# Recurrence of a two-block network: crossing products go in two turns that interleave straight blocks of one head pair with across blocks of the other

## What is computed

```python
def wkv7_scan(r, decay, k, v, kk, a):
    def step(S, inp):
        r_t, w_t, k_t, v_t, kk_t, a_t = inp
        s_kk = jnp.einsum('bhij,bhj->bhi', S, kk_t)
        S = (S * w_t[:, :, None, :] - s_kk[..., None] * (a_t * kk_t)[:, :, None, :]
             + v_t[..., None] * k_t[:, :, None, :])
        return S, jnp.einsum('bhij,bhj->bhi', S, r_t)
    ...

def token_mix(...):
    p = h @ w_in
    ...                                   # gated depthwise convolution u, layer norm, silu
    y = wkv7_scan(rh, heads(decay), kh, vh, kk, heads(a))
    y = layer_norm(y, LNX_EPS).reshape(B, T, RWKV_WIDTH) * lnx_g + lnx_b
    ...
    return jnp.concatenate([u, y], axis=-1) @ w_out

def second_block(x, ...):
    m = token_mix(...)
    x = x + gt_m * rms_norm(m, mix_post_g)
    f = channel_mix(h, w_up, ffn_dw_w, ffn_dw_b, w_down)
    x = x + gt_f * rms_norm(f, ffn_post_g)
```

## Time and profile before

| | us |
|---|---|
| median of 3 runs | 1750.25 |
| lowest, highest | 1749.92, 1757.47 |
| span of the profiled execution | 1749.1 |
| of it the recurrence, both halves (1159 to 1312.5) | 153.5 |

### The profile page before, as it was taken

One profiled execution on the slowest core, in us unless ns is written; L12 is line 12 of the kernel. 1 busy time (PEld: TensorE's weight loads), 2 busy tenths in 40 slices (PEclk: granted clock), 3 DMA queues, 4 the chain that ended last, 5 costly groups with the idle time before them and its releaser, 6 DMA issues.

```text
span 1749.1 us, 26683 instructions
## 1 busy us (share of the span) xinstructions
PE 1688.5 (97%) x10134; PEld 1366.6 (78%) x10134; DVE 959.1 (55%) x1408; ACT 429.0 (25%) x706; POOL 1014.4 (58%) x605
## 2 busy tenths in 40 slices
PE   7999999999989999999999999999999899999998
PEld 5888888887755678888888776878878788888886
DVE  5666551226656346655562168996756675565102
ACT  4000000016845321111100131223434333333000
POOL 2666667766576567666677743640005376666775
PEclk9999999999999999999999989999999899999998
DMA  5444443333220034444443322210002122322333
GB/s 188 153 146 144 144 145 119 99 117 99 81 76 2 12 107 157 142 145 146 146 150 109 99 88 65 86 61 3 3 2 85 60 95 97 96 96 96 105 101 108
DMA packets 48798, 173.76 MB, mean 99 GB/s; under 512 B 5424, under 2 KB 5808, under 8 KB 48464
## 3 DMA queue, kind: packets, MB, share of 16 engines
q1 hardware_dynamic: 39888, 143.00, 24.9%
q10 hardware_dynamic: 8832, 29.63, 5.3%
HBM read 170.51 MB, written 2.10 MB: 99 GB/s over the span
## 4 chain that ended last, share of the span: by engine, by line
PE 90%; DVE 3%; ACT 3%; POOL 2%; issue 1%; DMA 1%; SPq 0%; DVEq 0%; POOLq 0%; ACTq 0%
PE banks L591 24%; PE banks L593 24%; PE banks L592 24%; PE banks L971 4%; POOL prob L539 1%; PE banks L621 1%; PE banks L645 1%; PE banks L622 1%; PE banks L627 1%; PE banks L871 1%; PE banks L857 1%; PE banks L946 1%; PE banks L638 0%; PE banks L640 0%; PE banks L639 0%
## 5 line engine op out<-in xcount | busy, mean ns | idle before, releaser
L530 POOL TENSOR_SCALAR w_hi<-w_raw 128x1024 fp32r<-128x1024 f32 x260 | 291.4, 1121 | 656.1 <-DMA w_raw<-in_slabs 655.7
L532 POOL TENSOR_TENSOR w_lo<-w_raw,w_hi 128x1024 fp32r<-128x1024 f32 x260 | 643.7, 2476 | 21.7
L591 PE MATMUL banks<-h_hi,w_hi 128*128 128x512 f32 x1376 | 539.0, 392 | 2.5 <-POOL w_lo L532 2.5
L593 PE MATMUL banks<-h_hi,w_lo 128*128 128x512 f32 x1376 | 535.5, 389 | 0.0
L592 PE MATMUL banks<-h_lo,w_hi 128*128 128x512 f32 x1376 | 535.4, 389 | 0.0
L591 PEld LDWEIGHTS banks<-h_hi,w_hi 128*128 128x128 f32 x1376 | 258.3, 188 | 60.9 <-issue 4.5
L592 PEld LDWEIGHTS banks<-h_lo,w_hi 128*128 128x128 f32 x1376 | 258.4, 188 | 54.3 <-issue 1.2
L593 PEld LDWEIGHTS banks<-h_hi,w_lo 128*128 128x128 f32 x1376 | 258.3, 188 | 53.8
L591 PE MATMUL banks<-act_hi,w_hi 128*128 128x512 f32 x528 | 205.6, 389 | 0.0
L593 PE MATMUL banks<-act_hi,w_lo 128*128 128x512 f32 x528 | 205.4, 389 | 0.0
L592 PE MATMUL banks<-act_lo,w_hi 128*128 128x512 f32 x528 | 205.4, 389 | 0.0
(11 more groups left out here) (349 smaller groups left out, 1905.0 us busy)
## 6 DMA issues: line engine op xcount, KB each, us to landing
w_raw<-in_slabs SPq DMA_DIRECT2D x264, 512.0 KB, 3.5
adaw<-in_ada ACTq DMA_DIRECT2D x48, 512.0 KB, 3.6
xT<-in_x SPq DMA_DIRECT2D x2, 1024.0 KB, 7.0
relb<-in_relb ACTq DMA_DIRECT2D x8, 256.0 KB, 3.0
out_y<-xT SPq DMA_DIRECT2D x8, 256.0 KB, 2.1
block<-in_block ACTq DMA_DIRECT2D x1, 704.0 KB, 6.9
silc<-in_ada ACTq DMA_DIRECT2D x1, 512.0 KB, 6.0
tmp<-in_rope ACTq DMA_DIRECT2D x1, 512.0 KB, 4.0
```

The source lines that it names most:

```text
L530: nc.gpsimd.tensor_scalar(w_hi[:, r, :], w_raw[:, r, :], 1.0, 1.0, ALU.mult, ALU.mult).then_inc(S("w_hi"), 1)
L532: nc.gpsimd.tensor_tensor(w_lo[:, r, :], w_raw[:, r, :], w_hi[:, r, :], ALU.subtract).then_inc(S("w_split"), 1)
L591: mm(out, hi, rhs_hi, start=start, stop=False, skip_group_check=True)
L593: return mm(out, lo, rhs_hi, start=False, stop=stop, skip_group_check=True)
```

## The change

The crossing products are made by a new function, `crossed`, for both head pairs together, in two turns. In turn 0 the blocks are, chunk by chunk, the straight one of g0 and the across one of g1; in turn 1 the across one of g0 and the straight one of g1. Between the turns TensorE waits on `rk_crossed` until the last two blocks of both pairs are done. `begin_y` does the same for y. The plan's count is now kept for each pair by itself (`rk_mm0`, `rk_mm1`), and a crossed product counts 2, since its last two blocks each count 1. Both pairs' banks are waited for ahead of the first block, and for r4, r5 and rho both pairs' operands. Number and shapes of the matmuls stay the same, and so do the other engines' operations and their order.

```diff
+CROSSED = ("ar+p0", "mr+mt", "q0", "y1", "y2", "r4", "r5", "g+rho", "hd")
...
-                made += 1
+                made[g] += 2 if item in CROSSED else 1
...
+            def block_product(pairs, operands, result, b, parts, e, g, c, opens, opens_second):
+
+                p, n = result(e, c)
+                if parts == 2:
+                    out = bank[b + n // 4][CH * p:CH * p + CH, P * (n % 4):P * (n % 4) + P].rearrange("p (n t) -> p n t", n=2)
+                    opens = opens or opens_second
...
+            def crossed(pairs, operands, result, name, half):
+
+                taken = [free_banks(name, g, half) for g in range(2)]
+                for turn_ in range(2):
+                    if turn_:
+                        crossed_halves[0] += 4
+                        pe.wait_ge(S("rk_crossed"), crossed_halves[0])
+                    for c in range(NC):
+                        for g, (b, parts) in enumerate(taken):
+                            e = c % 2 ^ g ^ turn_
+                            last = block_product(pairs, operands, result, b, parts, e, g, c, turn_ == 0 and c // 2 == 0,
+                                                 turn_ == 0 and c // 2 == 2)
+                            if c >= NC - 2:
+                                last.then_inc(S(f"rk_mm{g}") if turn_ else S("rk_crossed"), 1)
...
                 for name, pair in (("p0", (mZ, rw)), ("mt", (k_, rw)), ("q0", (w_, mZ))):
-                    for across in range(2):
-                        for g in range(2):
-                            made([pair], by_feature, by_token, name, g, half, across)
+                    crossed([pair], by_feature, by_token, name, half)
...
-                    for across in range(2):
-                        for g in range(2):
-                            if across == 0:
-                                ready(f"rt{lvl}", g, half)
-                                ready(f"y{lvl}", g, half)
-                            made([(mP, mQ)], by_feature, by_token, "r4" if lvl == 1 else "r5", g, half, across)
+                    crossed([(off, mR)], by_token, by_feature, f"y{lvl}", half)
+                    for g in range(2):
+                        ready(f"rt{lvl}", g, half)
+                        ready(f"y{lvl}", g, half)
+                    crossed([(mP, mQ)], by_feature, by_token, "r4" if lvl == 1 else "r5", half)
...
-                for across in range(2):
-                    for g in range(2):
-                        if across == 0:
-                            ready("z", g, half)
-                        made([(mW, (in_h, 8, 2))], by_token, by_feature, "rho", g, half, across)
+                for g in range(2):
+                    ready("z", g, half)
+                crossed([(mW, (in_h, 8, 2))], by_token, by_feature, "rho", half)
```

More of the change, by code:

```diff
@@ L946, in turned_over @@
                     last = nc.tensor.transpose(bank[b][:, P * j:P * j + P], m[:, g, P * j:P * j + P], ident)
[L947 to L958, removed]
-                else:
[L960 to L972, removed]
-                if across == 0:
-                    last.then_inc(S("rk_straight"), 1)
-                else:
-                    last.then_inc(S("rk_mm"), 1)
@@ L978, in _ @@
[L978 to L985, removed]
+                last.then_inc(S(f"rk_mm{g}"), 1)
+            def block_product(pairs, operands, result, b, parts, e, g, c, opens, opens_second):
[3 more added lines that the diff above has]
+                    opens = opens or opens_second
+                else:
+                    out = bank[b][CH * p:CH * p + CH, CH * n:CH * n + CH]
+                for i, (lhs, rhs) in enumerate(pairs):
+                    r = two_blocks(*rhs, operands, e, g, c) if parts == 2 else block_of(rhs, operands, e, g, c)
+                    last = mm(out, block_of(lhs, operands, e, g, c), r, start=opens and i == 0, stop=i == len(pairs) - 1,
+                              skip_group_check=True)
+                return last
@@ new lines, in made @@
+            def made(pairs, operands, name, g, half):
+                b, parts = free_banks(name, g, half)
+                for j in range(NT):
+                    for e in range(2):
+                        for h in range(2):
+                            c = 2 * j + h
+                            last = block_product(pairs, operands, by_token, b, parts, e, g, c, j == 0 and e == 0, j == 2 and e == 0)
+                last.then_inc(S(f"rk_mm{g}"), 1)
+            crossed_halves = [0]
+            def crossed(pairs, operands, result, name, half):
[11 more added lines that the diff above has]
+                                last.then_inc(S(f"rk_mm{g}") if turn_ else S("rk_crossed"), 1)
@@ L1944, in move @@
             def move(name, half, g, ins):
[L1946 to L1947 removed]
+                dve.wait_ge(S(f"rk_mm{g}"), RK_PLAN[half, name, g][0])
+                made_of = ins(made_at(half, name, g))
+                if name not in ("ar", "mr"):
+                    made_of.then_inc(S("rk_" + name), 1)
             def masked(dst, src, mask, g):
@@ L2184, in _ @@
             recurrence(1)
-            dve.wait_ge(S("rk_mm"), RK_PLAN[1, "y", 1][0])
+            for g in range(2):
+                dve.wait_ge(S(f"rk_mm{g}"), RK_PLAN[1, "y", g][0])
             for j in range(4):
```

85 lines of the change are left out of this document (41 added, 44 removed).

## The result

| | before | changed |
|---|---|---|
| median of 11 runs each (us) | 1750.25 | 1760.13 |
| lowest, highest | 1748.45, 1757.47 | 1753.74, 1764.8 |
| span of the profiled execution | 1749.1 | 1762.9 |
| its mean granted clock | 0.985 | 0.976 |

The ratio is 1.005, with a 95% interval of 1.0038 to 1.0062. I had forecast 1745.7 and given 1742 to 1752, so the result lies outside the range, on the other side of no change. The profiled execution of the changed kernel is the slowest of its eleven, so its rows show the effect at its largest. Over the eleven, the mean clock is 0.980 in the median and 0.984 in the fastest (1753.74 us). From span to time 1.9 us pass.

A forecast was written before the change was run, and what follows sets the result against it. TensorE, busy for 97% of the span, was taken as the bound; -2.06 us in half 0 and -1.91 in half 1 made -4.0, with 0.5 from the clock -4.5, hence 1745.7 us, range 1742 to 1752.

The forecast's parts named there:

- The clock rival: Recurrence: one half-clock drop more or less costs or gains up to 1.7 us; under 1742 us by the clock, chance 0.06.
- a gain of 0.5 us: end_y of half 0: moving about 2 us ahead could save 1.2 us at full clock; half counted, 0.5.
- Four tiles at full pace: All crossing products: four tiles keep the two-tile pace side by side, 0.46 us per 64-column turn, 0.81 with 128.
- 64-column records get no faster: y, r, hd and y products: records stay at 29 ns, only 128-column ones speed up; 1761 us, chance 0.07.
- only two tiles at a time: Crossing products: tiles sharing rows or columns take turns, so 128-column products lengthen too; 1771 us, chance 0.04.
- the estimate from the floor of 25 ns: All matmuls: starts never closer than about 25 ns, giving about 1755 us; doubted because dense stretches show closer starts.
- The pause between turns: Between the two turns of each crossing product: 0.27 us, or 0.32 with 128 columns, at most 0.4.
- Part 1: p0 to q1: q1 starts 0.34 us later in half 0 and 0.35 us earlier in half 1.
- Part 2: y and r: half 0 nothing at level 1, -0.10 us at level 2; half 1 +0.36 and -0.12.
- Part 3: rho, hd and y up to the state chain: -2.3 us in half 0; -0.25 and -1.55 in half 1.
- The supply rival: hd and y: instruction supply tires to some 22 ns within a turn, losing about 0.45 us each; 1748 us, chance 0.16.

The follow-up runs named there:

- changed, with fillers: Changed kernel plus throwaway matmuls in TensorE's waits before mr+mt, q1 of half 0, each r4 and r5, and rho: 1750.15 us, ratio 1.0003 to the kernel before.
- the first part alone: Against the kernel before, only ar+p0, mr+mt and q0 go in two turns, the other products as before: 1752.76 us, ratio 1.002.
- filler kernel: Changed kernel with 6 filler matmuls before mr+mt, 7 before q1 of half 0, 7 before each r4 and r5, 5 before rho: 1750.15 us, ratio 1.0003.
- the fastest kernel: Against the kernel before, only rho, hd and y in turns, plus one filler matmul in each pause of both state chains: 1744.66 us, ratio 0.9969.
- the last part alone: Against the kernel before, only rho, hd and y go in two turns, without fillers: 1747.63 us, ratio 0.9979.

## Why the prediction was wrong

**The clock rival was priced in drops, and that is the step that failed.** I wrote that "TensorE now has more pauses at r4 and r5" and then allowed one drop of 3.4 us more or less, "up to 1.7 us". In the sum itself the clock stands only as a gain of 0.5 us. Yet my own times hold a wait of nearly 2 us ahead of r5 (the last start of y2 at 1202.23 + 1.19 = 1203.42, r5 at 1205.33), and I priced no drop behind it. I had tied the drops to the two state chains, which misreads: the one from 1290.0 on stands ahead of half 1's chain, behind the norm's statistics:

```profile
1286.39 3.77 PE L645 MATMUL banks<-both,tmp 128*128 128x1 f32 x32
```

What came is that by the granted clock the 153.5 us from 1159 on went from about 9 to 46 us at 1.2 GHz. From the first block of p0 to the last `centred`, the profiled executions take:

| | half 0 | half 1 | together |
|---|---|---|---|
| before | 68.7 | 75.0 | 143.8 |
| changed | 77.3 | 82.8 | 160.0 |
| changed, with fillers | 70.5 | 74.8 | 145.4 |

So of 16.3 us in the changed kernel's slowest execution 14.7 go away with the fillers, and at the median some 10. The Trainium skill (TensorE: Matmul & The Clock Gate, section "A second HAM failure mode: psum-queue depth-cycling") describes a kernel in which TensorE idles briefly between groups of matmuls and the clock swings between its two levels, so that the throughput suffers between the bursts. The trace of the changed kernel agrees, with waits of 1.65 to 2.04 us; that of the first part alone, with waits of 1.65 and 1.60 us and no drop behind them, shows that it need not come. I had read the page for its floor on matmul starts and not weighed this section.

**The rest: the turns at full clock.** The sum was also wrong by itself. The filler kernel against before gives its terms nearly without the clock (us, from the offsets of the same rows; minus is earlier):

| step | forecast | measured |
|---|---|---|
| q1, half 0 | +0.34 | +0.80 |
| y1 to y2, half 0 | 0 | +0.03 |
| y2 to z, half 0 | -0.10 | +0.29 |
| z to rho | 0 | +0.10 |
| rho to the chain | -2.3 | -1.53 |
| chain to p0 of half 1 | -0.5 | +2.10 |
| q1, half 1 | -0.35 | +0.02 |
| y1 to y2, half 1 | +0.36 | +0.83 |
| y2 to conv_mean | -0.12 | +0.29 |
| conv_mean to the statistics | -0.25 | -0.03 |
| statistics to the chain | -1.55 | -1.22 |
| chain to centred, half 1 | 0 | -0.07 |
| sum | -4.5 | +1.6 |

Of the 6.1 us between the two sums, 2.6 lie between the state chain and p0 of half 1, and the rest is spread over the products.

- *Four tiles at full pace* was right, for 2 to 3 us. A turn with 64 columns takes 0.69 - 0.22 = 0.47 us from first to last start, as forecast (0.46). The rival that 64-column records get no faster is refuted by this row, that of only two tiles at a time by p0's 2.35 us; that the first one's time, 1761, is nearly the time measured is chance, since at the clock of before the loss is gone. Refuted too is the estimate from the floor of 25 ns in the Trainium skill (the same page, section "Wait — 56ns, not 53.3ns?"): the burst of 126 records in 1.97 us doesn't agree with it where tiles alternate.
- *The pause between turns* was too small. From the last start of turn 0 (1196.13 + 0.47) to the first of turn 1 (1196.99) 0.39 us pass, not 0.27; VectorE follows p0 after 0.37, not 0.32, and ScalarE y2 after 0.33, not 0.27. That sits at the edge of the 0.4 that I had as a bound, but it recurs: y1 from first to last start is 1.33 us and not 1.19, p0 is 2.35 - 0.27 = 2.08 and not 1.94.
- *Part 1.* VectorE has ar 2.45 us after p0's start, not 2.26; mr+mt follows 0.26 us behind the second mask, not 0.11; and mr is masked 2.45 after that. Together 6.45 us, where I had 5.92. In half 1 these 0.5 us eat the whole gain that I had seen in the shorter q0.
- *Part 2.* That r4 of half 0 costs nothing, since "VectorE is busy with `factors` until 1200.32", held: the bonus sum behind r4 starts 0.28 us later after y1 (4.84 us in the filler kernel, against 4.56), but the transposes, which wait for VectorE, only 0.03 (5.83 against 5.80). The three other places (level 2 of half 0, both levels of half 1) lie 0.4 to 0.5 us above my terms. I had the wait for the last copy, but made it and the product behind it too short: r5 starts 3.37 us behind y2 in the filler kernel, not 3.10, and takes 1.33 to its last start, not 1.19.
- *Part 3.* The chain comes 7.31 us after rho in the filler kernel, 7.51 in the fastest kernel and 7.88 in the last part alone, where 8.84 was before and 6.5 my forecast. The last one has 0.91 us of supply pause in it (from 1217.58 to 1218.49); without that it is 6.97. My terms for half 1 add up to 8.57 us, not the 8.65 that I wrote, which changes little. The filler kernel has its pause later, 0.99 us inside the chain, which is half of the +2.10 behind it; the other half is one more drop there (6.8 us from 1224.9, not 3.4). Half 1 was right: the chain waits for VectorE's four products and not for y, at 12.71 us behind the statistics against 13.93.
- *The supply rival* had the right suspicion and the wrong form. I feared 22 ns within each turn and 0.45 us a turn. What happens is full speed and then one pause of 1 us or so in the long run of hd and y. That its time, 1748, is close to what the last products alone take (1747.63) is chance.

## What to carry to other kernels

Packing an in-order engine's work more densely was no gain here where another engine's moves lie between the pieces: the time goes into waits, and at y and r waits of 2 us between dense bursts cost TensorE its clock, far more than the waits themselves. Look at the granted clock of the stretch, fill the waits with matmuls that nobody reads as a test, and if the time comes back, keep the old order at those places and the new one only where products follow each other directly. Of any pace read over a few tenths of a microsecond, ask over how long a stretch it holds.

## What the hardware showed that I had not expected

- The granted clock fell to 1.2 GHz behind waits of only 1.65 to 2.04 us, and stayed there for up to 13.7 us while TensorE was busy for 10.47 of them. With 1.60 to 1.83 us of filler in them it stayed at 2.4 GHz. It need not fall behind them: with p0 to q0 alone in turns, waits of 1.65 and 1.60 us brought no drop.
- TensorE takes 128 pairs of weight load and matmul on four tiles in 1.97 us (15 ns a pair), then starts none for 1.6 to 2.0 us, once for each 16 KB fetched by the instruction queue; over the stream that is 31 ns a pair.
- Executions differ ahead of the recurrence: p0 of half 0 starts between 1162.3 and 1168.2 us in the thirteen profiled executions, whose work up to there is the same. A single profile can't rank kernels that differ by 5 us; the medians can.
